# An MLP in four quarters, three of whose up projections use Strassen's seven products

## What is computed

```python
for layer in range(2):
    ...                                       # mixer of the layer
    h = layer_norm(ALPHA * h + mix, ln_mix_g[layer], ln_mix_b[layer])
    hid = jnp.square(jax.nn.relu(h @ mlp_w_up[layer] + mlp_b_up[layer]))
    h = layer_norm(ALPHA * h + hid @ mlp_w_down[layer] + mlp_b_down[layer],
                   ln_mlp_g[layer], ln_mlp_b[layer])
return h[:, 16:, :]
```

## Time and profile before

| | us |
|---|---|
| median of 3 runs | 1367.02 (1365.03 to 1369.89) |
| the profiled execution, its time | 1364.11 |
| the profiled execution, its span | 1362.3 |
| mean granted clock of TensorE | 0.995 |
| PE / weight loads / DVE / ACT / POOL busy | 1312.8 / 1178.8 / 625.6 / 512.1 / 515.8 |

### The profile page before, as it was taken

One profiled execution on the slowest core, in us unless ns is written; L12 is line 12 of the kernel. 1 busy time (PEld: TensorE's weight loads), 2 busy tenths in 40 slices (PEclk: granted clock), 3 DMA queues, 4 the chain that ended last, 5 costly groups with the idle time before them and its releaser, 6 DMA issues.

```text
span 1362.3 us, 21811 instructions
## 1 busy us (share of the span) xinstructions
PE 1312.8 (96%) x9502; PEld 1178.8 (87%) x9502; DVE 625.6 (46%) x1052; ACT 512.1 (38%) x734; POOL 515.8 (38%) x220
## 2 busy tenths in 40 slices
PE   6999998999999999999999999999999999999996
PEld 5998855999999999999998988877788888888885
DVE  6999554456530024412356456465566300343125
ACT  4334487445222222222365245264453222223124
POOL 1001154355444444445544124114654444444440
PEclk9999999999999999999999999999999999999998
DMA  6221100222233322333221221212223333223321
GB/s 183 93 63 33 64 1 1 69 88 68 90 92 93 93 94 93 94 93 94 94 63 63 63 63 63 62 63 93 93 64 97 106 103 95 93 93 93 93 63 62
DMA packets 141791, 108.27 MB, mean 79 GB/s; under 512 B 8096, under 2 KB 139376, under 8 KB 141696
## 3 DMA queue, kind: packets, MB, share of 16 engines
q1 hardware_dynamic: 141296, 106.77, 25.9%
q10 hardware_dynamic: 400, 0.11, 0.0%
HBM read 104.77 MB, written 2.10 MB: 78 GB/s over the span
## 4 chain that ended last, share of the span: by engine, by line
PE 83%; ACT 7%; DVE 6%; issue 2%; DMA 1%; POOL 1%; SPq 0%; DVEq 0%; ACTq 0%
PE pb L706 63%; PE pb L872 2%; PE pb L718 2%; PE pb L873 2%; PE pb L874 2%; PE pb L812 1%; PE pb L813 1%; PE pb L750 1%; PE pb L811 1%; ACT wh L1289 1%; PE pb L1073 1%; DMA x_tok<-in_x 1%; DVE st L2313 1%; PE pb L982 1%; PE pb L1071 1%
## 5 line engine op out<-in xcount | busy, mean ns | idle before, releaser
L567 POOL TENSOR_TENSOR wl<-raw,wh 128x2048 fp32r<-128x2048 f32 x81 | 378.4, 4672 | 513.3 <-ACT wh L1289 513.1
L706 PE MATMUL pb<-hh,wh 128*128 128x264 f32 (+1 forms) x1160 | 301.6, 318 | 3.2 <-DVE qd L2295 1.6
L706 PE MATMUL pb<-hh,wl 128*128 128x264 f32 (+1 forms) x1160 | 296.9, 314 | 0.0
L706 PE MATMUL pb<-hl,wh 128*128 128x264 f32 (+1 forms) x1160 | 296.8, 314 | 0.0
L1289 ACT ACTIVATE wh<-raw 128x2048 fp32r<-128x2048 f32 x97 | 185.1, 1908 | 92.3 <-DMA raw<-in_mlp_w_down 62.2
L706 PEld LDWEIGHTS pb<-hh,wh 128*128 128x128 f32 x1160 | 190.7, 188 | 19.2 <-issue 3.7
L706 PEld LDWEIGHTS pb<-hl,wh 128*128 128x128 f32 x1160 | 190.6, 188 | 13.8 <-issue 1.2
L706 PEld LDWEIGHTS pb<-hh,wl 128*128 128x128 f32 x1160 | 190.5, 188 | 13.5
L706 PE MATMUL pb<-hidh,wh 128*128 128x264 f32 (+1 forms) x720 | 191.8, 321 | 0.0
L706 PE MATMUL pb<-hidh,wl 128*128 128x264 f32 (+1 forms) x720 | 191.0, 320 | 0.0
L706 PE MATMUL pb<-hidl,wh 128*128 128x264 f32 (+1 forms) x720 | 190.2, 318 | 0.0
(11 more groups left out here) (391 smaller groups left out, 2043.2 us busy)
## 6 DMA issues: line engine op xcount, KB each, us to landing
raw<-in_mlp_w_up SPq DMA_DIRECT2D x32, 1024.0 KB, 5.3
raw<-in_mlp_w_down SPq DMA_DIRECT2D x32, 1024.0 KB, 5.5
raw<-in_w_in_c SPq DMA_DIRECT2D x16, 1024.0 KB, 5.2
raw<-in_w_in_ab SPq DMA_DIRECT2D x8, 1024.0 KB, 5.5
raw<-in_w_out_ab SPq DMA_DIRECT2D x4, 1024.0 KB, 4.9
raw<-in_w_out_c SPq DMA_DIRECT2D x4, 1024.0 KB, 5.0
x_tok<-in_x SPq DMA_DIRECT2D x2, 1024.0 KB, 8.2
raw<-in_s_w_glu SPq DMA_DIRECT2D x1, 1024.0 KB, 5.4
```

Source lines behind the costliest of these rows:

```text
L567: pool.tensor_tensor(wl[:, c % RING, :], raw[:, c % RING, :], wh[:, c % RING, :].bitcast(F32), ALU.subtract).then_inc(w_lo, 1)
L706: mm = pe.matmul(pb[:, bank + b, 0:z_ - a], lhs, rhs[:, a:z_], start=first and hi and k == 0, stop=last and k == len(todo) - 1)
```

## The change

Each MLP now has four quarters of the hidden width, `up?0`, `down?0` to `up?3`, `down?3`, every stage with 4 slots and 8 tiles; a slot of `down` now holds 256 output features and 8 row chunks. The first quarter of `up` is computed as before. In the other three a slot (a block, 1024 rows of x by 256 features) is split in four quadrants of the weights (A11, A12, A21, A22: which half of the features, which half of the rows) and four of x (which half of the rows, which half of the tokens). Seven products of half size (4 chunks, 128 features, half of the tokens) are made in place of eight, in Winograd's form: three use quadrants and four use sums.

DVE forms the sums of the weights per block (`quad_sums`, one of them in place in `raw`), and once per layer the four sums of x (`x_sums`), all in float32; ACT makes their high parts (`quad_high`, and in `run` before tiles 5 and 6), DVE the low parts, those of the block's own weights too (`quad_low`, `x_low`), so POOL has nothing to do for these blocks. DVE also makes the low parts of the first two slots of `down` in quarters 1 to 3. PE runs the products of the four blocks in the order of `QUAD_ORDER` (block, product), over six banks. Product 1 is copied out by ACT (`m1_copy`), since it enters several results; DVE adds the others up out of PSUM (`u2`, `u3`, `c22`, `c21`, `c12`), and ACT applies bias, ReLU and square (`first`, `second`). The sum over quarters is kept in `h`: quarter 0 as before, quarters 1 and 2 by a DVE addition straight from PSUM, quarter 3 in the layer norm.

```diff
-        ("up00", 8, 16), ("down00", 8, 8), ("up01", 8, 16), ("down01", 8, 8),
+        *[(f"{w}0{q}", 4, 8) for q in range(4) for w in ("up", "down")],
         *layer1, ("g", 4, 8), ("out_c", 4, 8),
...
+QUAD_ORDER = [(0, 1), (0, 6), (0, 5), (0, 2), (0, 7),
+              (1, 1), (1, 6), (0, 4), (0, 3), (1, 5), (1, 2), (1, 7),
+              (2, 1), (2, 6), (1, 4), (1, 3), (2, 5), (2, 2), (2, 7),
+              (3, 1), (3, 6), (2, 4), (2, 3), (3, 2), (3, 7), (3, 5), (3, 4), (3, 3)]
+QUAD_BANKS = ((4, 5, 6), (7, 2, 3))
...
-LOWS_POOL = [c for c in range(NSLOTS) if c not in LOWS_DVE]
+LOWS_DVE = [*range(1, GLU), GLU + 1, GLU, *[STAGES[f"down0{q}"][0] + j for q in range(1, 4) for j in range(2)],
+            *range(G + 2, G + 6), *[STAGES[f"down1{q}"][0] + j for q in range(1, 4) for j in range(2)]]
+LOWS_POOL = [c for c in range(NSLOTS) if c not in LOWS_DVE and c not in QUAD_SLOTS]
...
-                for half in range(2):
-                    stream(f"up{layer}{half}", mlp_w_up[layer], col0=2048 * half)
-                    stream(f"down{layer}{half}", mlp_w_down[layer][2048 * half:2048 * (half + 1), :], P, 16)
+                for q in range(4):
+                    stream(f"up{layer}{q}", mlp_w_up[layer], col0=1024 * q)
+                    stream(f"down{layer}{q}", mlp_w_down[layer][1024 * q:1024 * (q + 1), :])
...
+                def quad_product(bank, weights, moving, first):
+
+                    o = pb[:, bank, 0:w]
+                    for kc in range(4):
+                        (lh, ll), (xh, xl) = weights(kc), moving(kc)
+                        pe.matmul(o, lh, xh, start=first and kc == 0, stop=False, skip_group_check=True)
+                        pe.matmul(o, lh, xl, start=False, stop=False, skip_group_check=True)
+                        mm = pe.matmul(o, ll, xh, start=False, stop=kc == 3, skip_group_check=True)
+                    return mm
...
+                for j, m in QUAD_ORDER:
+                    k, c = k0 + j, s0 + j
+                    p_, q_, r_ = QUAD_BANKS[j % 2]
+                    if m == 1:
+                        pe.wait_ge(a1_lo, k + 1)
+                        if k >= 2:
+                            pe.wait_ge(c11_out, k - 1)
+                        quad_product(p_, lambda kc: ring(c, kc, 0), lambda kc: x_half(kc, 0), True).then_inc(product, 1)
+                    if m == 6:
+                        pe.wait_ge(s_lo[0], k + 1)
+                        if k >= 2:
+                            pe.wait_ge(c21_out, k - 1)
+                        if j == 1:
+                            pe.wait_ge(*emptied(before, 7))
+                        quad_product(q_, lambda kc: summed_w(k, 0, kc), lambda kc: x_sum(1, kc), True).then_inc(product, 1)
+                    if m == 5:
+                        pe.wait_ge(a2_lo, k + 1)
+                        if k >= 2:
+                            pe.wait_ge(c12_out, k - 1)
+                        quad_product(r_, lambda kc: ring(c, kc, P), lambda kc: x_sum(0, kc), True).then_inc(product, 1)
+                    if m == 2:
+                        pe.wait_ge(m1_out, k + 1)
+                        quad_product(p_, lambda kc: ring(c, 4 + kc, 0), lambda kc: x_half(4 + kc, 0), False).then_inc(product, 1)
+                    if m == 7:
+                        pe.wait_ge(u2_out, k + 1)
+                        pe.wait_ge(s_lo[1], k + 1)
+                        quad_product(q_, lambda kc: summed_w(k, 1, kc), lambda kc: x_sum(2, kc), False).then_inc(product, 1)
+                    if m == 4:
+                        pe.wait_ge(a2_lo, k + 1)
+                        pe.wait_ge(u3_out, k + 1)
+                        quad_product(q_, lambda kc: ring(c, 4 + kc, P), lambda kc: x_sum(3, kc), False).then_inc(product, 1)
+                    if m == 3:
+                        pe.wait_ge(s_lo[2], k + 1)
+                        pe.wait_ge(c22_out, k + 1)
+                        quad_product(r_, lambda kc: summed_w(k, 2, kc), lambda kc: x_half(4 + kc, 1), False).then_inc(tile_done, 2)
...
+                    seen = 8 * (4 * layer + q)
+                    run(f"down{layer}{q}", hidh[layer], hidl[layer], lambda k: (hid_ready, seen + k + 1),
+                        order=[1, 0, 3, 2, 5, 4, 7, 6] if q else None, norm=2 * layer + 1 if q == 3 else None)
...
+                    if name[:2] == "up" and t in (5, 6):
+                        for i in (2 * t - 10, 2 * t - 9):
+                            act.wait_ge(t_summed, 4 * int(name[2]) + i + 1)
+                            act.activation(tth[:, 4 * i:4 * i + 4, 0:width(name)], traw[:, 4 * i:4 * i + 4, 0:width(name)],
+                                           ACT.Copy).then_inc(t_hi, 1)
...
+            def down(layer, q):
+
+                name = f"down{layer}{q}"
+                s0, _, t0, tiles = STAGES[name]
+                k = 4 * QUADS.index(f"up{layer}{q + 1}")
+                empty = into_tmp(name, ACT.Identity, lambda t: cols_b[:, 32 + 8 * layer + t:32 + 8 * layer + t + 1]) if q == 0 else None
+                for t in range(tiles):
+                    if q == 0:
+                        act.wait_ge(tile_done, t0 + t + 1)
+                        empty(t, dense(name, t), (t0 + t) % 2).then_inc(emptied_by["act"], 1)
+                    if t == 1:
+                        high(s0 + 2)
+                    if t == 3:
+                        high(s0 + 3)
+                    if t == 4:
+                        for part_ in ("a1", "a2", "s2", "s3", "s4"):
+                            quad_high(k, part_)
+                    if t == 6:
+                        for part_ in ("a1", "a2", "s2", "s3"):
+                            quad_high(k + 1, part_)
+                    if t == 7:
+                        quad_high(k + 1, "s4")
...
+                m1_copy(0)
+                for j in range(4):
+                    k = k0 + j
+                    c11(j)
+                    if j < 2:
+                        quad_high(k + 2, "a1")
+                    if j < 3:
+                        m1_copy(j + 1)
+                    if j < 2:
+                        quad_high(k + 2, "a2")
+                        quad_high(k + 2, "s2")
+                        quad_high(k + 2, "s3")
+                    if j == 2:
+                        high(s0 + 4)
+                    second(j)
+                    if j < 2:
+                        quad_high(k + 2, "s4")
+                    first(j)
+                high(s0 + 5)
...
+            def quad_sums(k, which):
+
+                c = QUAD_SLOTS[k]
+                wide = raw[:, c % RING, :].rearrange("p (k n) -> p k n", k=KC)
+                a11, a12, a21, a22 = wide[:, 0:4, 0:P], wide[:, 4:8, 0:P], wide[:, 0:4, P:256], wide[:, 4:8, P:256]
+                s2, s3, s4 = (s_raw(k, i).rearrange("p (k n) -> p k n", k=4) for i in range(3))
+                if which == "s123":
+                    dve.wait_ge(w_in[c % RING], 16 * (c // RING + 1))
+                    if k >= 2:
+                        dve.wait_ge(product, products_before(k - 2, 7))
+                    TT(s3, a11, a21, ALU.add).then_inc(s_summed[1], 1)
+                    dve.wait_ge(s_summed[1], k + 1)
+                    TT(a21, a21, a22, ALU.add).then_inc(s1_summed, 1)
+                    dve.wait_ge(s1_summed, k + 1)
+                    TT(s2, a21, a11, ALU.add).then_inc(s_summed[0], 1)
+                if which == "s4":
+                    if k >= 2:
+                        j = (k - 2) % 4
+                        dve.wait_ge(tile_done, STAGES[QUADS[(k - 2) // 4]][2] + 2 * j + 2)
+                    dve.wait_ge(s_summed[0], k + 1)
+                    TT(s4, s2, a12, ALU.add).then_inc(s_summed[2], 1)
...
+            def x_sums(name):
...
+                TT(r1, b11, b12, ALU.subtract).then_inc(t_summed, 1)
+                dve.wait_ge(t_summed, 4 * int(name[2]) + 1)
+                STT(r2, r1, -1.0, b22, ALU.mult, ALU.subtract).then_inc(t_summed, 1)
+                TT(t3, b22, b12, ALU.subtract).then_inc(t_summed, 1)
+                dve.wait_ge(t_summed, 4 * int(name[2]) + 2)
+                STT(t4, r2, -1.0, b21, ALU.mult, ALU.subtract).then_inc(t_summed, 1)
+
+            def x_low(name, i):
+
+                w = width(name)
+                dve.wait_ge(t_hi, 4 * int(name[2]) + i + 1)
+                TT(ttl[:, 4 * i:4 * i + 4, 0:w], traw[:, 4 * i:4 * i + 4, 0:w], tth[:, 4 * i:4 * i + 4, 0:w].bitcast(F32),
+                   ALU.subtract).then_inc(t_lo, 1)
...
+                    else:
+                        hc = cols(name, h[:, t, :])
+                        dve.wait_ge(tile_done, t0 + t + 1)
+                        TT(hc, hc, dense(name, t), ALU.add).then_inc(emptied_by["dve"], 1)
+                    if t == 4:
+                        quad_sums(k, "s123")
+                        quad_sums(k, "s4")
+                    if t == 5:
+                        for part_ in ("a1", "s2", "a2", "s3", "s4"):
+                            quad_low(k, part_)
```

(69 more changed lines are left out.)

248 lines of the change are left out of this document (222 added, 26 removed).

## The result

The changed kernel takes **1370.25 us** (median of 20 runs, 1368.55 to 1374.36), the kernel before 1367.03 in the runs beside it (20 runs, 1364.10 to 1370.04). The ratio is **1.0028, with a 95% interval of 1.0018 to 1.0038**. Twelve of every 96 half-size matmuls of three quarters of each up projection are gone, and the kernel is 0.3% slower. The profiled execution took 1373.75 us, with a span of 1371.7.

The account below looks back on a forecast made before the run. PE, busy 1312.8 of 1362.3 us, was taken as the bound. Terms -17.3 - 12.0 + 10.9 + 12.2 + 3.4 + 3.1 = +0.3 us, on the median's scale 1367.3 us; range 1349 to 1379.

Parts of the forecast that it names:

- the likeliest case: First quarter's handover: POOL holds DVE twice in each layer; 1367.3 us, range 1361 to 1373, chance 0.45.
- The case of 1345: First quarter's handover: POOL holds DVE in neither layer, stops of 1.7 and 2.8 us remain; 1345 us, chance 0.13.
- The matmuls removed: Strassen blocks in three quarters of up: fewer or shorter matmuls save 17.3 us in layer 0 and 12.0 in layer 1.
- A 256-column matmul costs about half of a 512-column one: Layer 1's blocks: pitch 0.1176 us against 0.2267; the skill's figures would give +41 in place of -12 us.
- Nothing on the path inside the blocks: Strassen blocks: DVE and ACT work stays ahead of PE with a margin of 1.5 us, so it costs nothing.
- the rival in which DVE comes late: Strassen blocks, product 4 of block 2: DVE late by 1.9 us in each of six quarters; 1379 us, chance 0.20.
- The handover: First quarter, up to down: PE waits for tile 7's hidden rows, +10.9 us in layer 0, +12.2 in layer 1.
- The clock: After the handover's stop in each layer: idle PE loses its clock, 1.7 us per layer, +3.4 in all (0 to 7).
- The norms: After each layer's last down tile: shorter halves start the norm's chain later, 1.1 plus 2.0 us, +3.1 (0 to 5.8).
- The down projections: Down stages of both layers: number of matmuls kept, so no change in time.

Follow-up runs that it names:

- the version with both edits: Changed kernel with the four lows of x behind tile 7's hidden operations and the lows of down's first two slots on VectorE: 1345.05 us (0.9845).
- the added work: The version with both edits, with the fourth weight sum repeated once or three times for blocks 2 and 3 of each Strassen stage: 1344.88 and 1364.20 us.
- one more edit: The version with both edits, with layer 1's rows of the sums of x 256 elements apart, no longer 264: 1343.24 us (0.9839).

## Why the prediction was right

Forecast 1367.3, no change within the noise; measured 1370.25, 3.2 us over the kernel before and inside the likeliest case's own range of 1361 to 1373. It was the right case: the stop came where it was laid out, and when its cause is lifted 25 us come back. But that the total came within 3 us owes something to luck. The blocks gave 3.0 us less than forecast and the handover cost 3.0 us less; these two errors cancel, and so do the two in the down projections. The case of 1345 (no collision) was not what the version with both edits showed, although the number is the same. That case keeps stops of 1.7 and 2.8 us and gives their clock no price. Its situation, the four lows in front and no collision, is the version with the lows of down on VectorE, and that took 1358.21: stops of 3.4 and 3.5 us (with one more operation of 2.3 in front of each), and 6.2 us of clock. With no stop at all the forecast's own terms give 1367.0 - 29.3 + 3.1 = 1340.8, and 1345.05 was measured. Step by step:

- **The matmuls removed, -17.3 and -12.0.** The scheme is worth 27.8 us by the medians and 26.7 by the traces. The pitch was taken too small: a stage of layer 0 takes 40.95 us and not 40.3, one of layer 1 39.88 and not 39.5, over six stages 3.0 us.
- **A 256-column matmul costs about half of a 512-column one.** 0.1187 against 0.2268 in the same kernel, 52%. By an estimate from the two figures of the Trainium skill (TensorE: Matmul & The Clock Gate, section Back-to-back issue gap), 81 ns at 128 and 131 ns at 512 columns, half the columns would have cost three quarters and layer 1 would have lost time; for this stream the trace disagrees.
- **Nothing on the path inside the blocks.** No wait there, so the rival in which DVE comes late (1379) did not occur. The margins laid out by hand were 2.0, 2.0 and 1.5 us, and the added work says 1.5 and, in layer 1, 1.2.
- **The handover, +10.9 and +12.2.** 10.0 and 10.1 (9.88 and a wait of 0.18 before it), by the mechanism forecast: two holds by POOL, then the lows of x, then tile 7. Layer 1 was set 2 us too high: counted from the stage's first POOL low, tile 7's rows were there after 1055.15 - 1024.01 = 31.1 us and not after 1048.6 - 1015.9 = 32.7. Together 20.1 and not 23.1.
- **The clock, +3.4.** 5.1. This term was mis-sized: I took 1.7 us per stop from a stop of 2.0 us; here a stop costs 2.0 to 3.2, in the changed kernel 3.1 and 2.0.
- **The norms, +3.1.** Between the end of the 51 (now 27) matmuls of the last tile's first stream and the next stage lay 721.25 - 668.29 = 52.96 us, and now 727.64 - 676.32 = 51.32. The second half has 24 fewer matmuls, 2.9 us, and 1.6 came through: 1.2 us lost. At the end of the run 27.73 us became 1371.7 - 1344.90 = 26.80: 2.0 lost. **3.2** in all, against 1.1 + 2.0.
- **The down projections, no change.** This failed, twice and in opposite directions. Layer 0 pays about 2.6 us (0.1217 for 0.1200, 1536 matmuls), layer 1 gets about 2.2. I had counted matmuls and not looked at where their rows stand.

Put together with what was measured: -29.3 + 3.0 (pitch in the blocks) + 20.1 + 5.1 + 3.2 + 2.6 - 2.2 = +2.5 us. The medians differ by 3.2, the two MLPs in the traces by 3.1.

## What to carry to other kernels

When a change takes work off the engine that bounds the kernel, look at the last thing that its queues do before the next stage starts: here the place of six operations, four in the queue and two on another engine, ate 25 of 28 us, and putting them elsewhere made the kernel 1.5% faster than before (1.6% with one more edit). Lay such a handover out by hand in time, queue by queue, with what one engine does to the other; a sum of busy times would have shown DVE with 40% to spare. And a change that isolates the gain (quarters without the scheme, the scheme without the wait) is worth more than the comparison of the two kernels, where both are hidden.

## What the runs showed of the hardware that was not expected

- The place of rows in SBUF changes the pitch of the matmuls that read them, by about 1.5% in layer 0 (0.1200 with rows 640 elements apart, 0.1217 at 528; 669 against 657 matmuls in 80 us) and up to 3% in layer 1 (0.2333 to 0.2268, with nothing else moved). It is not a matter of 128-byte alignment alone.
- After a stop, the cost in clock does not grow with its length: stops of 3.4, 5.3 and 10.0 us in layer 0 cost 3.0, 2.0 and 3.1 us, those of 3.5, 5.4 and 9.9 in layer 1 cost 3.2, 2.2 and 2.0.
- A DVE operation on two SBUF inputs that starts 0.1 us behind a POOL operation on two SBUF inputs waits until that one ends and then does its own work: 5.10 and 5.02 us for operations of 0.71 and 0.70, 5.58 for one of 1.25. With the weights' lows made by DVE in 2.3 us each in place of POOL's 4.6, the wait went from 10.0 to 3.4.
- Code that no edit touches took up to 4.9 us longer ahead of the MLP in one profiled execution than in another, and that goes with the clock. Where the granted clock from 160 to 240 us was 1.00 (seven executions), ACT's `wh` in the layer norm ahead of the first MLP starts at 307.7 to 308.5; where it was 0.96 (three), at 310.2 to 311.0; in the changed kernel it was 0.94, and it starts at 312.7. The estimates (1 - 0.96) x 80 = 3.2 and (1 - 0.94) x 80 = 4.8 us fit these steps. One of the three at 0.96 is the kernel before with only layer 1's hidden rows moved, so it does not come with the change. The twelfth execution (rows 528 apart) shows 0.95 nearly everywhere and starts at 311.7. What lowers the clock there was not tried.
